# A two-block sequence model on one core: order of the recurrence and the first attention units in the odd mixer, and six zero products

## The reference

```python
def odd_mixer(h, w_in, ..., w_out):
    z = h @ w_in
    lru_x, lru_gate, q, k, v = jnp.split(z, [...], axis=-1)
    xc = causal_dwconv(lru_x, lru_conv_w) + lru_conv_b
    y_lru = rg_lru(xc, ...) * jax.nn.gelu(lru_gate)
    y_att = dilated_attention(q, k, v, q_norm_g, k_norm_g)
    return jnp.concatenate([y_lru, y_att], axis=-1) @ w_out

def rg_lru(xc, w_a, b_a, w_x, b_x, lam):
    r = sigmoid(xb @ w_a + b_a)
    i = sigmoid(xb @ w_x + b_x)
    log_a = -LRU_C * r * softplus(-lam)
    a = exp(log_a)
    mult = sqrt(-expm1(2.0 * log_a))
    bt = mult * (i * xc)
    # hs[t] = a[t] * hs[t-1] + bt[t]
    return hs
```

## Time and profile before

| | |
|---|---|
| Median of 3 runs | 1758.34 us (1756.26 to 1758.51) |
| The profiled execution | 1758.6 us, its span 1756.8 us |
| PE busy | 1719.5 us, 98% |
| DVE busy | 1331.4 us, 76% |
| ACT busy | 999.3 us, 57% |
| POOL busy | 679.6 us, 39% |
| Mean granted clock of PE | 0.994 |
| DMA | 288.31 MB, mean 164 GB/s |

### The profile page before, as it was taken

How to read it: one execution, slowest core, us unless ns; L and a number is a source line. 1 busy time by engine, 2 the same in 40 slices (tenths; PEclk the granted TensorE clock), 3 DMA queues, 4 the chain that set the end, 5 groups by cost and what they waited for, 6 DMA issues and landing times.

```text
span 1756.8 us, 31885 instructions
## 1 busy us (share of the span) xinstructions
PE 1719.5 (98%) x12968; PEld 1632.8 (93%) x12968; DVE 1331.4 (76%) x1952; ACT 999.3 (57%) x1558; POOL 679.6 (39%) x417
## 2 busy tenths in 40 slices
PE   9989999988999999999999999999999999999997
PEld 8989999987999999999778999999999877899997
DVE  7758866566686859985797699777996599669794
ACT  6475544684654554576564566446477556366562
POOL 7631103961310166344474411037344366331113
PEclk9999999999999999999999999999999999999999
DMA  8435655541455554464345455555455235545552
GB/s 294 147 110 180 197 170 174 192 127 54 147 190 181 179 180 158 157 214 139 104 144 190 146 179 192 177 182 176 151 182 180 97 133 179 180 144 193 187 178 81
DMA packets 80930, 288.31 MB, mean 164 GB/s; under 512 B 9104, under 2 KB 9360, under 8 KB 80656
## 3 DMA queue, kind: packets, MB, share of 16 engines
q1 hardware_dynamic: 79776, 283.15, 48.3%
q10 hardware_dynamic: 1008, 3.11, 0.5%
HBM read 285.18 MB, written 1.05 MB: 163 GB/s over the span
## 4 chain that ended last, share of the span: by engine, by line
PE 93%; DVE 4%; ACT 2%; issue 1%; POOL 0%; DVEq 0%; ACTq 0%; POOLq 0%
PE lin L704 28%; PE lin L706 28%; PE lin L705 28%; PE stat L801 1%; PE stat L1198 1%; PE tr L1198 1%; ACT w_hi L1263 1%; PE logit L900 1%; PE logit L1161 1%; PE logit L1070 1%; PE logit L1092 1%; PE logit L994 1%; PE tr L911 1%; PE tr L1148 1%; PE lin L1018 0%
## 5 line engine op out<-in xcount | busy, mean ns | idle before, releaser
L1263 ACT ACTIVATE w_hi<-w_raw 128x1024 fp32r<-128x1024 f32 (+1 forms) x546 | 537.7, 1032 | 357.1 <-PE lin L706 356.1
L500 POOL TENSOR_TENSOR w_lo<-w_raw,w_hi 128x1024 fp32r<-128x1024 f32 (+1 forms) x197 | 472.4, 2411 | 340.6 <-ACT w_hi L1263 237.3
L500 DVE TENSOR_TENSOR w_lo<-w_raw,w_hi 128x1024 fp32r<-128x1024 f32 (+1 forms) x349 | 485.6, 1395 | 53.2 <-ACT w_hi L1263 52.2
L704 PE MATMUL lin<-h_hi,w_hi 128*128 128x256 f32 x1632 | 466.6, 286 | 2.8 <-DVE h_lo L509 2.2
L704 PE MATMUL lin<-hid_hi,w_hi 128*128 128x256 f32 x1616 | 460.9, 285 | 2.3 <-DVE hid_lo L509 1.7
L705 PE MATMUL lin<-h_lo,w_hi 128*128 128x256 f32 x1632 | 461.8, 283 | 0.0
L706 PE MATMUL lin<-h_hi,w_lo 128*128 128x256 f32 x1632 | 461.7, 283 | 0.0
L705 PE MATMUL lin<-hid_lo,w_hi 128*128 128x256 f32 x1616 | 457.2, 283 | 0.0
L706 PE MATMUL lin<-hid_hi,w_lo 128*128 128x256 f32 x1616 | 457.2, 283 | 0.0
L704 PEld LDWEIGHTS lin<-h_hi,w_hi 128*128 128x128 f32 x1632 | 313.2, 192 | 5.5 <-issue 3.9
L705 PEld LDWEIGHTS lin<-h_lo,w_hi 128*128 128x128 f32 x1632 | 313.3, 192 | 1.0 <-issue 0.7
(11 more groups left out here) (326 smaller groups left out, 2688.7 us busy)
## 6 DMA issues: line engine op xcount, KB each, us to landing
w_raw<-in_upA SPq DMA_DIRECT2D x112, 512.0 KB, 3.8
w_raw<-in_upB SPq DMA_DIRECT2D x64, 512.0 KB, 3.8
w_raw<-in_xbc SPq DMA_DIRECT2D x48, 512.0 KB, 4.1
w_raw<-in_dnA SPq DMA_DIRECT2D x32, 512.0 KB, 3.6
w_raw<-in_dnB SPq DMA_DIRECT2D x32, 512.0 KB, 3.7
w_raw<-in_z SPq DMA_DIRECT2D x32, 512.0 KB, 4.1
w_raw<-in_gates SPq DMA_DIRECT2D x32, 512.0 KB, 4.1
w_raw<-in_ps SPq DMA_DIRECT2D x32, 512.0 KB, 4.1
```

The lines of the kernel that those rows point to most:

```text
L500: eng.tensor_tensor(w_lo[slab.slot][:, half, part], w_raw[slab.slot][:, half, part], w_hi[slab.slot][:, half, part].bitcast(F32), ALU.subt ...
L704: nc.tensor.matmul(out, lhs[0], rhs[0], start=first, stop=False)
L1263: nc.scalar.activation(w_hi[slab.slot][:, half, part], w_raw[slab.slot][:, half, part], ACT.Copy)\
```

## The change

What it does:

- ACT: root(4) moves from behind square(5) to behind root(3), ahead of exp and tanh; exp and tanh move behind square(5). The square root of -m moves behind the copy of the first value slab and root(5).
- DVE: norm(4) runs ahead of the recurrence. mask(0) runs ahead of the recurrence's square and m; norm(5) and probs(0) run between m and the product with the square root; then come the scans and the gate product, and behind them mask(1) and mask(2). Before, the scans stood between mask(0) and probs(0), and norm(5) and the gate product between mask(1) and mask(2).
- PE: `warming` takes the tile that it writes. In the units 1, 2 and 7, which have no part of an output slab, PE issues two products of zeros into the bank of the second output slab, which is free then. The opening's 19 are unchanged.

```diff
-            def warming(products):
+            def warming(products, out):
 
                 pe.wait_ge(s.hid_split, 2)
                 for _ in range(products):
-                    nc.tensor.matmul(logit[:, 0, :], zeros[:, 0:P], zeros, start=True, stop=True)
-
-            warming(19)
+                    nc.tensor.matmul(out, zeros[:, 0:P], zeros, start=True, stop=True)
+
+            warming(19, logit[:, 0, :])
...
                 if 3 <= u <= 6:
                     half, k = (u - 3) // 2, (u - 3) % 2 * (NC4 // 2)
                     late_part(od_out[0], out_operand, range(k, k + NC4 // 2), OUT_LAST, wait_out_chunk, (half,))
+                else:
+                    warming(2, lin[od_out[1].bank][:, 0, :])
                 if u + 2 < UNITS:
                     at_logits(u + 2)
                 at_values(u - 1)
...
-                if n >= 1:
+                if 1 <= n <= 4:
                     qk_root(n - 1)
...
                 if n == 4:
+                    qk_root(4)
+                if n == 5:
                     act.wait_ge(s.lru_r, 1)
                     act.wait_ge(s.lam_chain, LAM_LINKS)
                     for func, out in ((ACT.Exp, lru_a), (ACT.Tanh, lru_th)):
...
                     ins.then_inc(s.lru_a, 1)
-                if n == 5:
-                    act.wait_ge(s.lru_m2, 1)
-                    nc.scalar.activation(lru_th[:, :, :], lru_m[:, :, :], ACT.Sqrt, scale=-1.0).then_inc(s.lru_mult, 1)
...
             v_copy(0)
             qk_root(COUNT["od_qk"] - 1)
+            act.wait_ge(s.lru_m2, 1)
+            nc.scalar.activation(lru_th[:, :, :], lru_m[:, :, :], ACT.Sqrt, scale=-1.0).then_inc(s.lru_mult, 1)
             at_exp(0)
...
-            for n in range(4):
+            for n in range(5):
                 qk_norm(n)
             dve.wait_ge(s.lru_i, 1)
             stage_released(dve, "od_lru")
             dve.wait_ge(s.lru_first, 2)
             lc.link(tt(lru_i[:, :, :], lru_i[:, :, :], lru_xc[:, :, :], ALU.mult))
+            at_mask(0)
             dve.wait_ge(s.lru_a, 1)
             lc.link(tt(lru_m[:, :, :], lru_a[:, :, :], lru_a[:, :, :], ALU.mult))
             stt(lru_m[:, :, :], lru_m[:, :, :], 1.0, lru_th[:, :, :], ALU.add, ALU.mult).then_inc(s.lru_m2, 1)
-            qk_norm(4)
+            qk_norm(5)
+            at_probs(0)
             dve.wait_ge(s.lru_mult, 1)
             lc.link(tt(lru_i[:, :, :], lru_i[:, :, :], lru_th[:, :, :], ALU.mult))
-            at_mask(0)
             for c in range(NC4):
                 ins = nc.vector.tensor_tensor_scan(lru_hs[:, c, :], lru_a[:, c, :], lru_i[:, c, :], 0.0, ALU.mult, ALU.add)
             lc.link(ins)
-            at_probs(0)
+            tt(lru_hs[:, :, :], lru_hs[:, :, :], lru_gate[:, :, :], ALU.mult).then_inc(s.lru_y, 1)
             at_mask(1)
-            qk_norm(5)
-            tt(lru_hs[:, :, :], lru_hs[:, :, :], lru_gate[:, :, :], ALU.mult).then_inc(s.lru_y, 1)
             at_mask(2)
```

## The result

The changed kernel takes 1765.2 us (median of 7 runs, 1763.7 to 1765.81) against 1758.34 us; the ratio is 1.0032, with a 95% interval of 1.0019 to 1.0045, that is 3.3 to 7.9 us slower with 5.6 in the middle. The forecast was +4.9 us and 1763.2 us. The medians differ by 6.9, and 1765.2 lies 0.2 above the upper end of the range; the ratio puts the changed kernel at 1764.0, inside it. Direction and mechanism were right, the size was low.

What follows compares the result with a forecast made beforehand. PE bounds the kernel (93% of the chain), with waits and low clock; 6.9 us won are given back, and late release, zero products and clock sum to +5.6 or +4.1, middle +4.9: 1763.2 us, range 1755.5 to 1765.0.

Steps and rivals of the forecast that it cites:

- Part 1: Slab 4, root(4) and norm(4) first: logits(0) at 389.7 instead of 394.52, PE gains 6.9 us by transposes(0).
- Part 2: DVE's recurrence beside POOL's splits delays mask(1): logits read at 411.05 or 409.55, 405.2 undisturbed; PE idle 5 to 7 us.
- the two orders: First POOL split against DVE's square of a, nearly a toss: POOL first gives mask(1) 411.05, DVE first 409.55.
- Part 3: Copy of v2 behind exp(1) on ACT lets PE go at 415.35 or 413.85: +2.05 or +0.55 us late.
- Part 4: Six zero products on PE: +0.87 us in unit 1, no cost in unit 2, +0.3 in unit 7.
- Part 5: Clock at half for 4.7 us after PE resumes: surcharge 2.35 us up to transposes(1), bounds nothing and 3.1.
- the bound of 3.1: Upper bound of the low-clock surcharge, if all PE work from release to transposes(1) is slow.
- (a): Rival: clock holds or comes back at once, surcharge 0 to 1.5; +1.8 to +4 us, middle +2.6, 1761; chance 0.20.
- (b): Rival: POOL not in DVE's way, mask(1) at 405.2; -2.6 to 0 us, middle -1.5, 1756.8; chance 0.15.
- (c): Rival: faster, the first 6.9 us stay for the greater part; -5.7 to -3.6 us, 1754; chance 0.10.
- (d): Rival: slab 4's mean reaches ACT late, first gain shrinks 1 to 2 us; +6 to +8 us, 1765.5; chance 0.05.
- The 1.38 us of drain: ACT table switches: the skill's drain could make mask(1) up to 1.4 us later; left out of the sum.

Runs made afterwards that it cites:

- Run 2: Changed kernel, but POOL splits the first and second output slab only after mask(1) has run; 1764.58 us, ratio 1.0027 to the kernel before.
- run 7: Changed kernel with ACT's copy of the third value slab ahead of exp(1); 1764.58 us, ratio 1.0021 to the kernel before.
- run 10: Run 6's order with run 9's splits, but scans ahead of mask(2) and gate product behind probs(1); 1757.89 us, ratio 0.9995 to the kernel before.
- run 4: Kernel before, with the zero products in units 1, 2 and 7 and nothing else; 1759.83 us, ratio 1.0002 to the kernel before.
- run 1: Changed kernel without the six zero products in units 1, 2 and 7; 1765.78 us, ratio 1.0038 to the kernel before.
- run 3: Changed kernel with 14 more calls of zero products ahead of logits(2) and 5 behind them; 1761.57 us, ratio 1.0009 to the kernel before.
- run 9: Changed kernel, POOL splitting the first output slab when m is done, the second when mask(1) has read the logits; 1759.52 us, ratio 1.0001 to before.
- run 12: Run 11 with three calls of zero products behind logits(2) and three in unit 2 ahead of logits(4); 1753.24 us, ratio 0.9969 to the kernel before.
- run 6: Changed kernel without zero products, mask(1) ahead of probs(0), scans and gate product behind mask(2) and probs(1); 1756.3 us, ratio 0.9977 to before.
- run 11: Run 10 with the scans behind mask(2) and probs(1) again, no zero products; 1754.85 us, ratio 0.9979 to the kernel before.

## Why the prediction was right, and where it was short

**Part 1** held to 0.1 us: logits(0) 389.75 (389.7), logits(1) 396.55 (396.45), transposes(0) 403.89 (403.8). Its 6.9 us were there, and were given back.

**Part 2** held: of the two orders POOL went first, by 0.22 us (0.2), m was done at 397.4 (397.6), and mask(1) had read the logits at 410.83 (411.05). Run 2 shows the price of the turn-taking at 5.4 us, the term had it at 5.85 (411.05 - 405.2). The scans, which I counted as undisturbed, were so here only because no split was due; runs 7 and 10 show that they take part as well.

**Part 3** held: PE was let go at 415.04 (415.35).

**Part 4** held at full clock (run 4: 1.00, predicted 1.17) and did not hold where they stood: the call in unit 1 took 2 us, and the calls bought about as much back (run 1: 0.23 net).

**Part 5 is the term that was mis-sized.** I gave the low clock 4.7 us after the release and 2.35 us of cost. It lasted 7.7 us after the release, and run 3 measures 3.59 us for all of it: 2.94 up to transposes(1), near the bound of 3.1, and 0.65 in transposes(1) themselves (1.12 and 0.62 instead of 0.66 and 0.38) and behind, which the sum did not reach. That is 1.24 us too little. The middle of the two orders on POOL was 0.75 us below the branch that came. Against these stand the zero products, 0.17 too dear, and the release of PE, 0.42 too late (2.05 counted, 1.63 in the trace). Together this makes 1.4 of the 1.56 us between +4.9 and the trace's +6.46.

The step that failed is the length of 4.7 us, which I took over from the kernel before as if it went with the chip and not with the case. A second wait does not explain the difference: run 7 has none, PE works from 412.89 on without a gap, and the clock stays at half until 424.1, which is 11.2 us.

```profile
412.89 1.65 PE L994 MATMUL logit<-arena 64*128 64x128 f32 x6 [8.01 <-DVE arena L1994]
```

```profile
418.00:423.50 5.50, 5.50 (x20) 4.07 (x18) 1.01 (x2) 1.02 (x3) 0.00 (x0) 0.50 0.00 0
424.50:427.00 2.50, 2.50 (x23) 2.21 (x22) 0.43 (x2) 1.03 (x3) 0.00 (x0) 1.00 0.04 7
```

What sets the length stays open. PE works on a value slab in the kernel before and on the units' small products in run 7, and no run separates that from chance.

**Rivals.** (a), the clock holds: refuted by the granted clock of 0.50, and run 3 gives what it would have been (+2.87, within its +1.8 to +4). (b), POOL not in the way: refuted by the 2.72 and 2.84 us, and run 9, which comes nearest to it (mask(1) has read the logits 23.2 us after the mean, 23.1 given), has +1.9 in the trace and not the middle of -1.5: PE waits 1.1 and 3.2 us, much as (b) had it, but the clock then stays at half for 10 us, which (b) counted only as "some slow clock". (c) and (d) did not come; run 12 shows that -5.7 was to be had, by moving the recurrence, timing the splits and filling two gaps. By the prediction's own numbers the upper end of its range, +6.8, is 1765.1 and not 1765.0. The 1.38 us of drain for each table switch, which the Trainium skill gives ("ScalarE: Activation LUTs", What ACT_TABLE_LOAD costs), did not show: exp ran at 399.88, right behind its load, which began at 398.59 and took 1.28.

What also stays open: why the clock fell at 409 in run 6 after waits of at most 1.3 us, and held in the units of the kernel before with waits of 1.2 us. Runs 3 and 12 show only that it holds when the gaps are filled. How far the time at half clock varies between executions of one kernel, one trace of each can't show; the mean clock of the kernel before went from 0.991 to 0.995 in the 30 executions beside runs 1 to 4.

## What to carry to other kernels

When a late step of one queue is put first, ask for each step that it is put ahead of who waits for it next: here the 6.9 us that PE won were lost where it next needed DVE's mask. Moving the recurrence behind the masks turned the loss into a gain of 1.7 us, and of 5.7 with the splits and the clock seen to as well. Place large two-operand DVE work and POOL work against each other in time, as carefully as work on one engine; one wait on POOL was worth 4.6 us here. Count a long wait of PE twice, once as itself and once as the low clock after it, give that clock a wide bound, and fill gaps that can't be closed with products of zeros, which cost at most 0.2 us there and 1 us where PE had work.

## What the runs showed of the hardware that I had not expected

- Scans over SBUF take turns with POOL's splits: four took 2.44 alone, 3.92 beside one half and 5.51 beside two. A scaling of 384 columns by a scalar went from 0.42 to 1.71. A mask that reads PSUM and a reciprocal did not slow down (0.95, 3.35).
- The low clock lasted 13.7 us (409.1 to 422.7) around a wait of 6.5 us and one of 2.5, and 6.8 us around the 4.1 us of the kernel before. Counted from the end of the wait, it was 4.7 us there, 4.4 in run 11 (wait 2.5), 11.2 in run 7 (8.0) and 13.7 in run 10 (4.7, and one of 1.2 after it): the longer wait did not always have the longer low clock.
- Early rounding is not free: the copy ahead of exp(1) (run 7) released a split that cost DVE 1.5 us.
